# A two-block diffusion network on one core: norm sums collected in PSUM, square roots on ScalarE, and the low halves of three weight blocks on VectorE

## What is computed

```python
def rms_norm(x, g):                     # six times, in the first block
    y = x32 * rsqrt(mean(x32 * x32) + 1e-6)
    return y * g
def modulate(h, shift, scale):
    return h * (1 + scale) + shift
x = x + gate * stage(modulate(rms_norm(x, g), shift, scale))

def layer_norm(x, g, b):                # five times, in the second block
    xc = xf - mean(xf)
    return xc * rsqrt(mean(xc * xc) + 1e-5) * g + b
h = layer_norm(x, ln_in_g, ln_in_b)
for l in range(2):
    h = layer_norm(ALPHA * h + mixer(h) @ w_out, ln_mix_g, ln_mix_b)
    h = layer_norm(ALPHA * h + conv_ffn(h) @ w_down, ln_ffn_g, ln_ffn_b)
```

## Time and profile before

| what | value |
|---|---|
| median of 3 runs | 3731.72 us (3729.14 to 3734.68) |
| the profiled execution | 3734.95 us, its span 3733.2 us |
| TensorE busy | 3505.1 us (94%) |
| VectorE, ScalarE, GpSimd busy | 1916.7, 1265.7, 373.7 us (51%, 34%, 10%) |
| mean granted TensorE clock | 0.966 of full speed |
| HBM traffic over the span | 93 GB/s |

### The profile page before, as it was taken

The page is one execution under the profiler, slowest core; times in us unless marked ns, Lnnn a source line. Parts: engine busy times, 40 slices in busy tenths (PEclk is TensorE's granted clock), DMA queues, the critical chain, the costliest instruction groups (busy, mean ns, idle before and its releaser), DMA issues.

```text
span 3733.2 us, 40477 instructions
## 1 busy us (share of the span) xinstructions
PE 3505.1 (94%) x17064; PEld 2896.1 (78%) x17064; DVE 1916.7 (51%) x2662; ACT 1265.7 (34%) x1779; POOL 373.7 (10%) x216
## 2 busy tenths in 40 slices
PE   2999999899979999999999999989999998999998
PEld 2888888788767888788777888766788876678887
DVE  8433343566656453635344333486564538656464
ACT  4322122444433222322234222334342432344242
POOL 3311001111110000000001000420100033010001
PEclk9999999899989999999999999989999999999999
DMA  5423241011115353535212232210232222012221
GB/s 193 141 80 123 85 152 63 29 35 35 34 63 174 124 198 113 190 122 176 89 66 96 92 101 96 82 53 6 68 106 97 96 74 75 6 52 98 99 96 57
DMA packets 95798, 348.83 MB, mean 93 GB/s; under 512 B 10624, under 2 KB 11136, under 8 KB 95104
## 3 DMA queue, kind: packets, MB, share of 16 engines
q1 hardware_dynamic: 94320, 343.06, 27.6%
q10 hardware_dynamic: 1296, 3.18, 0.2%
HBM read 344.10 MB, written 2.10 MB: 93 GB/s over the span
## 4 chain that ended last, share of the span: by engine, by line
PE 84%; DVE 9%; ACT 4%; POOL 1%; issue 1%; DMA 0%; SPq 0%; ACTq 0%; DVEq 0%; POOLq 0%
PE PS L341 83%; DVE CAC L1872 2%; ACT G L1111 1%; DVE ST L1679 1%; PE PS L413 1%; DVE WL L1448 1%; POOL SM L2160 1%; DVE SCR L1479 1%; ACT HH L994 1%; ACT G L982 1%; DVE PTL L1662 1%; DVE X L1843 0%; ACT PTH L1092 0%; DVE ST L1963 0%; DVE SCR L1471 0%
## 5 line engine op out<-in xcount | busy, mean ns | idle before, releaser
L341 PE MATMUL PS<-HH,WH 128*128 128x512 f32 (+1 forms) x3120 | 1194.4, 383 | 46.8 <-DVE HL L1560 21.1
L341 PE MATMUL PS<-HL,WH 128*128 128x512 f32 (+1 forms) x3120 | 1177.9, 378 | 0.0
L341 PE MATMUL PS<-HH,WL 128*128 128x512 f32 (+1 forms) x3120 | 1174.6, 376 | 0.0
L1448 DVE TENSOR_TENSOR WL<-RAW,WH 128x1024 fp32r<-128x1024 f32 x462 | 580.9, 1261 | 895.3 <-ACT WH L943 895.2
L943 ACT ACTIVATE WH<-RAW 128x1024 fp32r<-128x1024 f32 x496 | 523.2, 1057 | 1217.2 <-PE PS L341 1206.9
L341 PEld LDWEIGHTS PS<-HH,WH 128*128 128x128 f32 x3120 | 595.4, 191 | 164.0 <-DVE HL L1560 23.3
L341 PEld LDWEIGHTS PS<-HL,WH 128*128 128x128 f32 x3120 | 595.3, 191 | 109.4 <-issue 5.5
L341 PEld LDWEIGHTS PS<-HH,WL 128*128 128x128 f32 x3120 | 594.0, 190 | 108.7
L341 PE MATMUL PS<-AH,WH 128*128 128x512 f32 x1392 | 525.9, 378 | 1.7 <-DVE WL L1448 1.7
L341 PE MATMUL PS<-AL,WH 128*128 128x512 f32 x1392 | 525.5, 377 | 0.0
L341 PE MATMUL PS<-AH,WL 128*128 128x512 f32 x1392 | 523.8, 376 | 0.0
(11 more groups left out here) (277 smaller groups left out, 3288.2 us busy)
## 6 DMA issues: line engine op xcount, KB each, us to landing
RAW<-wst SPq DMA_DIRECT2D x640, 512.0 KB, 3.3
X<-xT SPq DMA_DIRECT2D x1, 2048.0 KB, 12.2
out<-X SPq DMA_DIRECT2D x8, 256.0 KB, 2.0
PTF<-cb SPq DMA_DIRECT2D x1, 1024.0 KB, 4.8
Y<-yT SPq DMA_DIRECT2D x1, 1024.0 KB, 6.9
PTF<-cb ACTq DMA_DIRECT2D x1, 1024.0 KB, 4.8
HM<-sg ACTq DMA_DIRECT2D x4, 256.0 KB, 3.7
ROPE<-rope SPq DMA_DIRECT2D x1, 512.0 KB, 4.5
```

Of the source, the lines that this page charges most:

```text
L341: return e.matmul(o, l, r, start=start, stop=stop)
L1448: e.tensor_tensor(lo, raw_block(s), f32(hi), ALU.subtract).then_inc(*did("dve_done", ("wlo", b)))
```

## The change

All eleven norms are rewritten; the stages between them keep their work.

- Sums over tiles go to PSUM: `means` multiplies each source by a column of 1/1024 and accumulates in one place with start and stop flags, so the result is a mean. The part that is ready early (`squares`, and `second` in `center`) is put between the last matmuls of tile 7 (`between`). Behind the last tile, only the square of tile 7 (RMS norm), or X(7) and its square (layer norm), are left. In f01, tiles 4 to 7 are summed directly from their squares and GpSimd adds only tiles 1 to 3.
- ScalarE takes the square root, with eps as bias and reading PSUM; VectorE takes the reciprocal. A dummy activation (`prepare`) makes ScalarE load the table of the square root while tile 7 runs, and the next function's table after the norm.
- The scale is folded in VectorE's multiplication (scalar_tensor_tensor) and the shift in ScalarE's write of the high half and in VectorE's low half. Layer norm then writes `X(k)` + shift in eight extra ScalarE instructions after the norm.
- The first mean of a layer norm is that of X(0) to X(3) with divisor 1024, doubled; it is made in tile 5 by one matmul with 128x512 result; tiles 5 to 7 are shifted before their last addition, so nothing is subtracted after it.
- In the last output tile, block splitting goes only up to `upto["mid", tile]`, and the rest is done inside the norm, from its third or fourth tile on. VectorE does no splitting ahead of its statistics in the norm.
- `lane = True` stands behind the first `lin` of a mixer, so the low halves of its first three blocks are made by VectorE.
- The activation of the second conditioning vector is moved behind norm f01.

```diff
+        def means(name, src, n, step, start, stop, *more, into=None):
+            if start:
+                claim(name)
+                _, prior = hold(("st", name), 512, into, ("pnread", name))
...
+            for t in range(n):
+                m = mm(bank["st", name][:, t:t + 1], src[:, t * 128:(t + 1) * 128], mean, start and t == 0, stop and t == n - 1)
...
         def norm(st):
-            stat(st, [(ACC, 128, ones, ("acc", up, 6)), (G(("sq", up, 7)), 128, ones, ("sq", up, 7))], nt, 1,
-                 ("gdone", ("sq", up, 7)))
-            spread(st, nt, None, ("rs", st))
+            for m in range(4, 8) if up == "at" else (7,):
+                means(st, G(("sq", up, m)), N // 128, ("sq", up, m), False, m == 7, ("gdone", ("sq", up, m)))
+            spread(st, N // 128, None, ("rs", st))
...
+            def first():
+                bk, prior = take(("mean", st), NX)
+                q.wait_ge("sum", st)
...
+                mm(bk[:, :], mean.broadcast_to([128, 128]), ACC[:, 0:512], True, True).then_inc(*did("pe_done", ("tile", ("mean", st))))
+            def second():
+                means(("v", st), A2t, 4, ("csq", st, 6), True, False, into=7)
+                means(("d", st), ACC, 4, ("cadd", st, 6), True, False, ("acc read", st), into=6)
+            return {5: {(at[0], 0): first}, 7: {(at[1], 0): second}}.get(m, {})
...
         def layer_norm(st):
+            means(("d", st), X(7), 4, ("x", BEFORE[st], 7), False, True)
+            means(("v", st), G(("ce", st, 7)), 4, ("csq", st, 7), False, True, ("gdone", ("ce", st, 7)))
+            spread(("d", st), 4, None, ("dmean", st))
+            spread(("v", st), 4, None, ("rs", st))
...
-            lane = True
             lin([(("b0", l), hs(1536), NX), (("b1", l), q1_kr, NX), (("b2", l), hs(1728), NX)], xs)
+            lane = True
...
+        def prepare(fn, *step):
+            q.wait_ge("eps")
+            e.activation(LM[:, 6:7], EP[:, 0:1], fn).then_inc(*did("act_done", ("ready", *step)))
...
+            e.activation(sm(st, 0, n), bank["st", st][:, 0:n], ACT.Sqrt, bias=EP[:, 0:1]).then_inc(*did("act_done", ("std", st), ("pnread", st)))
...
-                e.activation(hview(k, N)[0], s[:, 0:N], ACT.Copy).then_inc(*did("act_done", ("hhi", st, k)))
+                a = e.activation(hi[:, 0:512], s[:, 0:512], ACT.Identity, bias=mcol(l, 3 * i, k, 0))
...
+                if k >= 2:
+                    part(upto[LAST[st]], 1)
+            if st in FFNS:
+                prepare(ACT.Silu, "silu", st)
...
+            prepare(ACT.Sigmoid if st[0] == "m" else ACT.Silu, "next", st)
+            for k in range(8):
+                q.wait_ge("h", st, k)
+                e.activation(X(k), X(k), ACT.Identity, bias=v2(b, k)).then_inc(*did("act_done", ("ln", st, k)))
...
+            e.reciprocal(sm(st, 16, n), sm(st, 0, n)).then_inc(*did("dve_done", ("rs", st)))
...
-            e.tensor_tensor(sm(name, b, n), sm(name, a, n), MH[:, 0:n], ALU.pow).then_inc(*did("pool_done", ("rs", name)))
```

More of the change, by code:

```diff
@@ L52 @@
 KS = (2, 3, 4, 5, 6, 0, 1, 7)
+AFTER = {before: stage for stage, before in BEFORE.items()}
 def wide(stage):
@@ L352, in lin @@
             K = len(xs)
+            for t in tiles:
+                upto["mid", t[0]] = allowed()
             for k, (hi, lo, step, rows) in enumerate(xs):
@@ L452, in ffn @@
                 for m in range(8):
-                    lin([(("d", st, p, m), [W(dn, l, f * 128, m * 128) for f in range(f0, f0 + nf)], N)], axs)
-                    if st == "f11" and p == 1 and m == 6:
-                        center("m0")
+                    between = {}
+                    if f0 + nf == FT:
+                        if st == "f11":
+                            between = center("m0", m, (1, 10))
+                        elif m == 7:
+                            between = {(nf - 2, 0): lambda: squares(AFTER[st])}
+                    lin([(("d", st, p, m), [W(dn, l, f * 128, m * 128) for f in range(f0, f0 + nf)], N)], axs, None, between)
         def attention(xs):
@@ L691, in fourier_out @@
             for m in range(4, 8):
[L692 to L712, removed]
+                lin([tile(m)], fx, None, {(6, 0): lambda: squares("f11")} if m == 7 else {})
@@ L895, in conv_ffn @@
                 for m in range(8):
-                    lin([(("cd", l, p, m), [W("ffn_w_down_2", l, j * 128, m * 128) for j in range(f0, f0 + 11)], NX)], axs)
-                    if p == 1 and m == 6:
-                        center("end" if l else "m1")
+                    lin([(("cd", l, p, m), [W("ffn_w_down_2", l, j * 128, m * 128) for j in range(f0, f0 + 11)], NX)], axs, None,
+                        center("end" if l else "m1", m, (1, 10)) if p else {})
         modulation(16)
         upto["start"] = 17 + NHL - 1
+        squares("f00")
         ffn("f00", norm("f00"))
@@ L909, in _ @@
         mods_on = True
-        xs = norm("f01")
-        ffn("f01", xs)
+        squares("f01")
+        ffn("f01", norm("f01"))
         ffn("f10", norm("f10"))
@@ L1018, in ffn @@
                 for m in range(8):
-                    if p == len(parts) - 1:
+                    last = p == len(parts) - 1
+                    if last and m == 7:
+                        stream(upto["mid", ("d", st, p, m)])
+                        prepare(ACT.Sqrt, "sqrt", AFTER[st])
+                    if last:
                         if st != "f11":
@@ L1585, in ffn @@
                         q.wait_ge("x", up, m)
-                    last = p == len(parts) - 1
                     steps = [("x", st, m)] if last else [] if N > 512 else [("xp", st, p, m)]
+                    if st == "f11" and last and m >= 5:
+                        steps.append(("cx", "m0", m))
                     if N == 512:
@@ L1598, in ffn @@
                         stream(upto["d", st, p, m])
-                    if st == "f11" and last and m == 6:
-                        center("m0")
         def lam():
@@ L1859, in layer_norm @@
+                if k and st != "end":
+                    hi, lo = hview(k - 1, NX)
+                    q.wait_ge("hhi", st, k - 1)
+                    e.scalar_tensor_tensor(out=lo, in0=X(k - 1), scalar=v2(shift, k - 1), in1=f32(hi), op0=ALU.add, op1=ALU.subtract).then_inc(
+                        *did("dve_done", ("h", st, k - 1)))
+                if k >= 3 and st != "end":
                     part(upto[LAST[st]], 1)
```

349 lines of the change are left out of this document (194 added, 155 removed).

## The result

| | before | after |
|---|---|---|
| median of the runs beside each other | 3732.15 us | 3704.01 us (3693.96 to 3705.07, 4 runs) |
| ratio | | 0.9919, 95% interval 0.9900 to 0.9938 |
| profiled execution, its span | 3734.95, 3733.2 us | 3704.28, 3702.4 us |

The change takes off 28 us of a forecast 35, inside the range of 3683 to 3715. The changed kernel was timed once more with the experiments: 3700.10 us (3697.10 to 3702.84) beside 3735.31, ratio 0.9908 (0.9893 to 0.9923), 35 us.

What follows compares the result with a forecast made beforehand. TensorE's dense matmuls bound the kernel, with the norms' chains of small steps as holes between them. The eleven norms' terms summed to -35.0 us, taking the median from 3731.7 to 3697 us, range 3683 to 3715.

Steps and rivals of the forecast that it cites:

- What bounds the kernel: Whole kernel: dense matmuls with holes between; a norm costs its chain's length, so moving work off it pays one to one.
- the low halves moved to VectorE: Three blocks' low halves, 1.26 us each, in tiles 5 to 7 ahead: cost nothing; without that cover 3.8 us.
- RMS norms with 512 tokens: Norms f10, fo, f11: shorter chain less about 1.0 us for the inserted sum; -2.7, -2.4 and -1.8 us.
- The price of the power: GpSimd's power in f10's chain, replaced by root and reciprocal: read as taking 1.92 us.
- Wide norms: Norms f00 and at: shorter head of chain, 2.4 us each, less 1.4 for sums in at; -2.3 and -1.0 us.
- f01: Norm f01: GpSimd adds less, TensorE sums more, chain about 2 us shorter; -2.0 us, with -6 as other end.
- m0 and m1: Layer norms before the mixers: chain 6 us shorter, less 0.2, 1.2 and 1.2 us in charges; -3.4 us each.
- No wait over 1.5 us for ScalarE's squares: Sign at the start of a mixer: no TensorE wait over 1.5 us for ScalarE's squares.
- c0 and c1: Layer norms c0 and c1: shorter chain, plus -1.2 us each for the first mean; -7.5 and -7.2 us.
- Sums in tile 7: Layer norms' 16 sum instructions among tile 7's dense matmuls: cost 2 x 1.0 us, with no wait before them.
- the first, part of the gain given back with the low clock: Rival: low clock at shorter pauses and tile 7 waits give back 12 to 20 us; 3709 to 3717; chance 0.18.
- ScalarE as the bound (the slower case): Rival: behind layer norms, 6.9 us of added ScalarE work per norm delays weight blocks; 3741 us; chance 0.04.

Runs made afterwards that it cites:

- r0_after: The changed kernel unaltered, timed and profiled again with the experiments; 3700.10 us, ratio 0.9908 to the kernel before.
- e1: Changed kernel with the low halves of each mixer's first three weight blocks back on GpSimd; 3700.78 us, ratio 0.9910 to the kernel before.
- yardstick: The same run as r0_after: the unaltered changed kernel, against which the other experiments are compared; 3700.10 us, ratio 0.9908.
- e3: Changed kernel with the root of the eleven norms back on GpSimd's power, the added constant on VectorE; 3703.45 us, ratio 0.9921.
- e8: Changed kernel with e2's and e4's edits, Silu's load moved in f00 and f01's sums reordered; 3672.54 us, ratio 0.9839.
- e4: Changed kernel with the early sums run behind the last W matmul, not within the last tile; 3688.08 us, ratio 0.9875.
- e2: Changed kernel with ScalarE's eight writes of X before each mixer moved behind the mixer's first sigmoid; 3697.34 us, ratio 0.9900.
- e10: Changed kernel with ScalarE's two writes a tile back in ten norms and no eight writes after layer norms; 3694.83 us, ratio 0.9898.

## Why the prediction was right, and where its terms were off

What each norm gave (its gap with the stage ahead, less the mixer's first stretch, which is booked with its own layer norm), us against the kernel before:

```
            f00    at   f01   f10    fo   f11    m0    c0    m1    c1   end   sum
forecast   -2.3  -1.0  -2.0  -2.7  -2.4  -1.8  -3.4  -7.5  -3.4  -7.2  -1.3  -35.0
after      -3.0   0.0  -3.1  -2.8  -1.8  -1.5  -0.5  -5.4  -0.6 -11.1  -1.0  -30.8
r0_after   -1.8  -0.4  -5.3  -2.4  -1.7  -2.1  -1.6  -8.5  -2.2 -11.1  -1.2  -38.3
```

- **What bounds the kernel, and that a chain is paid one to one**: right. The gaps shrank by 36.6 us, and the low halves moved to VectorE were free, as said (e1).
- **RMS norms with 512 tokens**: forecast -6.9 for the three, measured -6.1 and -6.2. The forecast chain of f10 was 0.6 too long, mainly the spread (1.24 against 1.6), and the stages that the sums were put into grew by 1.3 to 1.6 (yardstick: 0.3 to 2.1) against 1.0. The price of the power was taken from the one norm in which it was disturbed; since the whole row of steps was replaced by measured ones, the sum did not depend on it, but my expectation of e3 did, and fell.
- **Wide norms**: -3.3 forecast, -3.0 and -2.2 measured. The gap of at gained 3.1 and not 2.4, but the stage f00 gave back 3.0 and 2.3 us: it waits for modulation products, and the early Silu load had been put ahead of them in ScalarE's queue. I had priced that load only behind the layer norms. The stage is 2.9 shorter in e8, with 0.8 of that in e4 already.
- **f01**: -2.0 forecast, -3.1 and -5.3 measured. The sums began 3.96 us after TensorE was free, and ran at the full clock at first.
- **m0 and m1**: the term that was priced worst. I charged 1.2 us each for ScalarE's backlog; the wait was of that size (1.3), but the mixer's first stretch grew by 4.3 and 4.0 us in the profile of after and by 2.7 and 2.5 in the yardstick, the rest of it with the granted clock. e2 shows the writes as the cause of the wait; that they cause the low clock behind it is likely from e10, which has none there, but is not shown, as e10 changes the norm as well. "No wait over 1.5 us for ScalarE's squares" came out as I wrote it, and was the wrong thing to look at.
- **c0 and c1**: -14.7 forecast, -16.5 and -19.6 measured, c0 less and c1 more in the profile of after. The chain kept 10.1 and 9.1 us in c0 and not 8.2, as two spreads of eight matmuls take 3.7 us. For the first mean I had -1.2 each (3.1 us where it was 5.9, less two late sums). But behind the mixer's first stretch, m1 is 6.0 us shorter in both profiles, and m0 0.9 and 3.0 (6.3 in e10, 7.8 in e8). What I had no term for is the low clock inside the mixers. Behind the first stretch TensorE is at half speed for 34.1 us in both mixers of the kernel before. In m1 it is 23.9 after, in both profiles; in m0 it is 34.1 in the one and 30.7 in the other. Half of these differences, as an estimate of what they are worth, is 5.1 us in m1, and 0 and 1.7 in m0; without them the change gave 0.9 to 1.3 in each mixer.
- **Sums in tile 7**: as priced, 2 x 1.0, and without a wait. What I did not ask was what TensorE does right behind that tile. e4 answers: it waits, and the sums would have been nearly free there. That is 12 us, more than any term of my sum.
- **The rivals**: the first, part of the gain given back with the low clock, is what happened in m0 and m1, at some 6 us beyond what I had charged and not 12 to 20. ScalarE as the bound (the slower case) showed its beginning and never reached the weight blocks.
- **Luck**: the total came out well in part because errors cancel. In the profile of after, m0 and m1 together fell 5.7 us short of the forecast and c1 went 3.9 beyond it, by about as much as the clock gave in the stage ahead of it, for which I had no term.
- **Open**: how much of the gain is the sums in PSUM, the folded scale and shift, or the splitting moved behind the statistics was not tested one by one.

## What to carry to other kernels

Short work that must be done before a dense stage ends is not free inside the stage; look first at the wait that follows the last dense product, and fill that. Before a small step is moved to a faster engine, check whether another row of work already covers it, and price it from more than one row. An engine that gets work "behind" a chain delays what its in-order queue holds next, and a wait of about 1 us on TensorE can come with a stretch at half speed that costs more than the wait (4.3 and 2.7 us in two profiles, for waits of 1.35 and 1.04).

## What was not expected of the hardware

The same kernel, profiled twice, gave these two lines of span and mean granted TensorE clock. First after, then r0_after:

```profile
core 0: 3702.4 us, clock 0.969
```

```profile
core 0: 3695.1 us, clock 0.973
```

The clock fell in both at the same kinds of place, behind short sums and pauses, but for stretches of different total: I add up 232.5 us at half speed in the one and 205.1 in the other. Stage m0 differs by 3.8 us between them with identical instructions. 1.6 of the 3.8 lie in the mixer's first stretch, and the two stages spend 44.4 and 39.2 us at half speed. That is as large as what several edits here are worth. A gain under 5 us was therefore read from gaps and stages and not from medians, and in the stages m0 and m1 even these do not settle it unless the time at half speed is set beside them. What decides the length of such a stretch stays open.

GpSimd's power took 1.92 us in place of 1.02, and a VectorE subtraction 2.75 in place of 0.75, where the other of the two engines had begun on a weight block 0.17 us earlier. A table load of 1.28 us was followed by its activation at once, in every place read where that activation had nothing else to wait for (1485.61 to 1486.90).
